# One more gate unit ahead of the delta heads of a hybrid attention and DeltaNet block, and its logits over more rounds

## What is computed

```python
h    = rmsnorm(x, pre_norm_gain) * (1 + scale) + shift          # scale, shift, gate from c @ w_ada
proj = h @ w_in                                                  # 1024 x 10840
# branch A: 8 heads of 128; an indexer of 8 heads of 64 picks 128 keys per query
score = einsum(w_idx, relu(q_idx @ k_idx.T * 64**-0.5)) ; causal ; top 128
y_a  = (softmax(q @ k.T over the chosen keys) @ v * silu(az)) @ w_a_out
# branch B: gated DeltaNet, 8 heads of 128, causal conv of width 4, silu, l2norm
y_b  = (rmsnorm(delta_rule(q, k, v, g, beta)) * silu(bz)) @ w_b_out
y    = sigmoid(ga) * y_a + sigmoid(gb) * y_b
out  = x + gate * rmsnorm(y @ w_o, post_norm_gain)
```

## Time and profile before

| | us |
|---|---|
| median of three runs | 810.59 |
| the profiled execution | 810.23 |
| its span, first to last instruction | 808.3 |
| TensorE busy | 776.9 |
| VectorE busy | 445.3 |
| ScalarE busy | 336.3 |
| GpSimd busy | 398.1 |
| granted TensorE clock, mean | 0.995 |

### The profile page before, as it was taken

How to read it: one execution, slowest core, us unless ns; L and a number is a source line. 1 busy time by engine, 2 the same in 40 slices (tenths; PEclk the granted TensorE clock), 3 DMA queues, 4 the chain that set the end, 5 groups by cost and what they waited for, 6 DMA issues and landing times.

```text
span 808.3 us, 11722 instructions
## 1 busy us (share of the span) xinstructions
PE 776.9 (96%) x4288; PEld 628.5 (78%) x4288; DVE 445.3 (55%) x998; ACT 336.3 (42%) x719; POOL 398.1 (49%) x348
## 2 busy tenths in 40 slices
PE   4998998999999899999999999999999999999997
PEld 4877875677877688878888777778777788878997
DVE  5858778767588977878754243243334233331114
ACT  5576544533544345444344433443432332222131
POOL 3665542365545455565435255365355355434451
PEclk9999999999999999999999999999999999999999
DMA  8945555433344142323122121222132245432602
GB/s 326 415 153 192 161 102 199 109 120 105 99 93 107 66 112 92 105 66 117 57 76 78 53 78 54 78 79 76 55 103 69 90 163 179 153 130 83 230 1 105
DMA packets 69496, 95.55 MB, mean 118 GB/s; under 512 B 32936, under 2 KB 45608, under 8 KB 69440
## 3 DMA queue, kind: packets, MB, share of 16 engines
q1 hardware_dynamic: 69440, 94.81, 36.0%
HBM read 85.02 MB, written 9.22 MB: 117 GB/s over the span
## 4 chain that ended last, share of the span: by engine, by line
PE 79%; DVE 10%; ACT 4%; DMA 3%; issue 2%; POOL 1%; SPq 1%; DVEq 0%; POOLq 0%; ACTq 0%
PE ps L735 19%; PE ps L737 18%; PE ps L736 18%; PE ps L1025 2%; PE ps L1079 2%; PE ps L1078 2%; PE ps L1077 2%; PE ps L1012 2%; ACT prob L1346 2%; DVE prob L1989 1%; DVE binv L1876 1%; DMA mod_rows<-in_w_mod 1%; PE ps L1019 1%; PE ps L867 1%; PE ps L852 1%
## 5 line engine op out<-in xcount | busy, mean ns | idle before, releaser
L1444 POOL TENSOR_TENSOR w_lo<-raw,w_hi 128x512 fp32r<-128x512 f32 x210 | 282.0, 1366 | 295.0 <-ACT w_hi L1097 294.9
L735 PE MATMUL ps<-h_hi,w_hi 128*128 128x512 f32 x648 | 274.9, 424 | 0.0
L737 PE MATMUL ps<-h_hi,w_lo 128*128 128x512 f32 x648 | 254.6, 393 | 0.0
L736 PE MATMUL ps<-h_lo,w_hi 128*128 128x512 f32 x648 | 254.0, 392 | 0.0
L735 PEld LDWEIGHTS ps<-h_hi,w_hi 128*128 128x128 f32 x648 | 122.5, 189 | 30.3 <-issue 9.1
L737 PEld LDWEIGHTS ps<-h_hi,w_lo 128*128 128x128 f32 x648 | 122.1, 188 | 27.5
L736 PEld LDWEIGHTS ps<-h_lo,w_hi 128*128 128x128 f32 x648 | 122.8, 190 | 22.0 <-issue 2.2
L1097 ACT ACTIVATE w_hi<-raw 128x1024 fp32r<-128x1024 f32 x105 | 109.6, 1054 | 17.1 <-PE ps L1079 17.1
L1282 ACT ACTIVATE o_tok<-ps 128x128 f32<-128x128 f32 x32 | 8.9, 277 | 90.5 <-PE ps L977 90.4
L1994 DVE SCALAR_TENSOR_TENSOR oat<-ps,za 128x512 f32<-128x512 f32 x8 | 5.5, 691 | 56.1 <-PE ps L1025 56.1
L1078 PE MATMUL ps<-w_lo,y_hi 128*128 128x256 f32 x128 | 36.2, 283 | 0.0
(11 more groups left out here) (280 smaller groups left out, 1367.9 us busy)
## 6 DMA issues: line engine op xcount, KB each, us to landing
raw<-in_w_units SPq DMA_DIRECT2D x105, 512.0 KB, 3.3
mod_rows<-in_w_mod SPq DMA_DIRECT2D x16, 512.0 KB, 8.7
inverse_tiles<-zero SPq DMA_DIRECT2D x12, 344.0 KB, 5.0
ada<-in_w_gate SPq DMA_DIRECT2D x8, 512.0 KB, 4.5
x_sb<-in_x SPq DMA_DIRECT2D x4, 512.0 KB, 6.1
first_raw<-in_w_first SPq DMA_DIRECT2D x8, 256.0 KB, 7.3
L<-gc_rows SPq DMA_DIRECT2D x8, 256.0 KB, 3.9
lower_tiles<-L SPq DMA_DIRECT2D x8, 256.0 KB, 2.3
```

The lines of the kernel that those rows point to most:

```text
L735: pe.matmul(out_ap, w_hi[:, slot, k, :], rhs_hi(k), start=(k == 0), stop=False)
L736: pe.matmul(out_ap, w_hi[:, slot, k, :], rhs_lo(k), start=False, stop=False)
L737: mm = pe.matmul(out_ap, w_lo[:, slot, k, :], rhs_hi(k), start=False, stop=(k == KT - 1))
L1444: ins = pool.tensor_tensor(w_lo[:, slot, ks], raw[:, slot, ks], w_hi[:, slot, ks].bitcast(F32), ALU.subtract)
```

## The change

`N_EARLY` goes from 5 to 6: GA 5 stands ahead of delta head 0, in rounds 52 to 55, and all of `R_DELTA` grows by 4 (52 to 56, ..., 164 to 168). With it go K 7, the grams of heads 4 to 7, the second inverse and its corner steps, the selection, `R_ROPE[0]` (151 to 155), `R_MASK` and `R_ATT[0]` to `R_ATT[2]` (192, 202, 212 to 196, 206, 216). The number of rounds, the units from AQ 1 on and `R_ATT[3]` on, the other ropes, and everything up to round 49 but the logits keep their rounds.

The extra units behind the heads are K 7, GA 6, GA 7, AV 0, AQ 0, AK 0, AZ 0 instead of K 7, GA 5, GA 6, GA 7, AQ 0, AK 0, AV 0, with AZ 0 behind head 7. AZ 0 so goes from rounds 176 to 179 to 164 to 167, AV 0 from 160 to 163 to 116 to 119.

The 12 pairs of logits go from rounds 38, 39, 40, 41, 43, 44, 45, 46, 48, 49, 50, 52 to 38, 39, 41, 42, 44, 45, 47, 48, 50, 51, 53, 55. The load of `P_b` for head 0 goes from round 47 to 51, that of the first inverse from 52 to 54.

```diff
-N_EARLY = 5
-MIDDLE = [("K", 4), ("GA", 0), ("K", 5), ("GA", 1), ("K", 6), ("GA", 2), ("GA", 3), ("GA", 4)]
-EXTRA = ([("K", 7)] + [("GA", n) for n in range(N_EARLY, KT)] + [("AQ", 0), ("AK", 0), ("AV", 0), ("AZ", 0)])[:HEADS - 1] + [None]
+N_EARLY = 6
+MIDDLE = [("K", 4), ("GA", 0), ("K", 5), ("GA", 1), ("K", 6), ("GA", 2), ("GA", 3), ("GA", 4), ("GA", 5)]
+EXTRA = ([("K", 7)] + [("GA", n) for n in range(N_EARLY, KT)] + [("AV", 0), ("AQ", 0), ("AK", 0), ("AZ", 0)])[:HEADS - 1] + [None]
...
-R_LOGIT = [R_DELTA[0] - 14 + 14 * (m // 2) // 11 for m in range(24)]
+R_LOGIT = [R_DELTA[0] - 18 + 17 * (m // 2) // 11 for m in range(24)]
```

## The result

Over 20 runs of each kernel the changed one has a median of 812.81 us (810.64 to 817.31), the one before 810.47 us (809.05 to 812.49). The ratio is 1.0035, 95% interval [1.0023, 1.0047]: slower by 0.35%, 2.8 us (the two medians stand 2.3 apart). The profiled execution of the changed kernel took 814.17 us, with a span of 812.3, so it stands 1.4 us above its median, where the profiled execution of before stood near its own.

The account below looks back on a forecast made before the run. TensorE, busy 776.9 of 808.3 us, was the bound; only gaps and slow clock could change. Terms 0.1 + 0.5 + 0.4 + 0.1 + 0.9 = +2.0 on 810.23 gave 812.2, stated as 812.4; range 811.0 to 813.4, eight in ten 808.8 to 814.3.

Parts of the forecast that it names:

- gaps at the logits: TensorE's three waits for VectorE's scoring, 3.07 us together, fall to between 0 and 0.6; 0 taken.
- end of corner step 7: On VectorE, this step ends at 144.2 (142.4 to 145.1) instead of 150.48.
- from there to the gram: From corner step 7's end through DMA queue, GpSimd and ScalarE to kd, ahead of head 4's gram: 12.9 us.
- gap before the gram: TensorE, due at 153.9, waits for kd until 157.1 before head 4's gram: 3.2 us (1.4 to 4.1).
- lost to the slow clock in this stretch: A half-speed stretch behind the gap before the gram costs 1.7 us, as one did behind the earlier 2.00 us gap.
- K1 of head 6 (AZ 0): AZ 0's VectorE product at round 168 delays the selection and makes K1 wait 0.5 us (0 to 0.6).
- rope 1 at head 7: Rope 1 at round 191, now between st2 and r3, costs 0.4 us (0 to 1.1), GpSimd's half included.
- rope 2 at attention 1: Rope 2 at round 207, between attention 1's second and third row maximum on VectorE, adds 0.9 us (0 to 1.1).
- The query decay: Head 0's P_b load falls behind the corner stores on the DMA queue, delaying kd; TensorE waits 3.2 us at head 4's gram.
- (a): Faster side: P_b barely late, a gap of 1.1 at head 4's gram, no slow clock; 808.4 or median 808.8; chance 0.17.
- (b): Neighbours' slack hides the three tail costs: 810.3 to 811, no change; chance 0.25.
- (c): The moved 2.04 us gap at head 2 is followed by a slow stretch: +1.7, 814.1; chance 0.18.

Follow-up runs that it names:

- experiment 3: Changed kernel with head 0's P_b load back in round 47, ahead of the corner stores, and ropes 1 and 2 four rounds later: 805.94 us, ratio 0.9948.
- 10: The same kernel as experiment 3, run again beside 9 on one chip: 806.12 us, ratio 0.9941 to the kernel before.
- 1: Changed kernel with only head 0's P_b load put back in round 47, ahead of the corner stores: 809.69 us, ratio 0.9991 to the kernel before.
- 4: Kernel before with only head 0's P_b load moved behind the corner stores, in round 50: 819.84 us, ratio 1.0117.
- experiment 5: Changed kernel with ropes 1 and 2 four rounds later and P_b left late: 809.44 us, ratio 0.9994 to the kernel before.
- 9: Kernel before with only the logit pairs respread, over rounds 38 to 52: 805.71 us, ratio 0.9943.
- 6: Changed kernel with P_b early and rope 2 alone four rounds later: 806.68 us, ratio 0.9955 to the kernel before.
- experiment 2: Changed kernel with the logit pairs kept in rounds 38 to 52, as before: 819.70 us, ratio 1.0114 to the kernel before.
- 7: Changed kernel with P_b early and the logit pairs kept in rounds 38 to 52: 814.55 us, ratio 1.0048 to the kernel before.
- 8: Changed kernel with P_b early, ropes 1 and 2 four rounds later and rope 0 in round 182: 805.43 us, ratio 0.9941 to before.

## Why the prediction was right, by its steps

The sum said 812.2 for an execution and 812.4 as a median; it was 814.2 and 812.8, slower as forecast and for the reason given. The agreement of the medians is closer than that of the terms. Term by term, in the profiled execution:

| term | forecast, us | measured, us |
|---|---|---|
| gaps at the logits | 0 (0 to 0.6) | 1.11 |
| end of corner step 7 | 144.2 | 144.97 |
| from there to the gram | 12.9 | 13.4 |
| gap before the gram | 3.2 | 3.52 |
| lost to the slow clock in this stretch | 1.7 | 3.0 |
| K1 of head 6 (AZ 0) | 0.5 | 0.31 |
| rope 1 at head 7 | 0.4 | 1.13 |
| rope 2 at attention 1 | 0.9 | 1.10 |
| AZ 1 at attention 0 | 0.1 | 0 |
| gaps in heads 1 and 2 | 0 | -1.6 |
| first logit products reached | 0 | -0.5 |

The last two rows: the gaps of 1.04 at 251.6 and 1.15 at 279.0 before are 0.23 and 0.40 after, and TensorE came to the logits at 114.32 instead of 114.84. Together: 1.11 + 3.52 - 3.07 = 1.56 for the gaps, 3.0 - 1.7 = 1.3 for the clock, 2.54 for the tail, less 1.56 and less 0.5, are 3.3; the spans differ by 4.0, and the 0.7 between is not assigned.

Luck has a part. The gap before the gram came out within 0.3 because both of its ends were late, TensorE by 1.0 (154.9 for 153.9) and `kd` by 1.3 (158.4 for 157.1). The 1.6 us that heads 1 and 2 gave back stand in no term of the forecast; without them the profiled execution would have stood at 815.7. The two gaps together are 0.6 to 1.6 us in the seven profiles with the changed kernel's rounds for the logits and 1.6 to 2.6 in the other five, so they may hang on the change, but they also differ within one kernel (1.25 in experiment 3, 0.70 in 10). Their cause is open.

Of the signs that the forecast named, the gap before the gram, its chain and the 2.2 us at attention 1 came as said; K1 of head 6 waited 0.31 and not half a microsecond, and the logits kept a gap over 0.6.

**The query decay** was right in place and order and near in size, and experiments 1 and 4 show it from both sides. The chain was 0.5 longer than summed because P_b took 4.25 us to land and be used instead of 3.76.

**The logits.** The step that failed here is "the three gaps fall to between 0 and 0.6": one of 1.11 stayed. VectorE in the changed kernel (the counterpart of the earlier trace rows), and beside it the same step in experiment 5:

```profile
120.79 2.31 DVE L1800 SCALAR_TENSOR_TENSOR kraw<-ps,pcol,kraw 128x511 f32<-128x511 f32 x3 [1.46 <-ACT kraw L1195]
...
123.70 1.75 DVE L1876 TENSOR_TENSOR binv<-pair_c,pair_a 128x512 f32<-128x512 f32 x1 [0.59 <-DMA pair_b<-inverse_tiles]
```

```profile
121.18 2.31 DVE L1801 SCALAR_TENSOR_TENSOR kraw<-ps,pcol,kraw 128x511 f32<-128x511 f32 x3 [1.45 <-ACT kraw L1196]
...
123.41 0.68 DVE L1877 TENSOR_TENSOR binv<-pair_c,pair_a 128x512 f32<-128x512 f32 x1
```

The taps began at 120.8, earlier than the 121.4 forecast, but corner step 0 then waited 0.59 for its DMA and ran beside GpSimd's split, 1.75 instead of 0.68, and pair 2 ended 1.1 late. In experiment 5 the same instruction met neither and pair 4 waited for nothing. Which it is varies from execution to execution: experiments 3 and 10 are the same kernel, the first without this gap, the second with 1.11. So 1.1 belonged in the bounds. The forecast also took 1.52 as the longest such product; that was the longest of eight (those from `pair_c`), and one from `pair_b` took 1.75 before too. The two waits met took 1.75 and 1.79.

**Rope 1** was mis-sized by 0.7. The sum followed VectorE: `r3` a little late, V3 not at all, as it turned out. The gap came on GpSimd (the first four lines are the changed kernel's, the last the kernel before's):

```profile
435.28 3.43 POOL L1532 TENSOR_TENSOR qk<-qk,tab_cos 32x1024 f32<-32x1024 f32 x1 [2.16 <-DVE sw L1955]
...
438.68 3.50 POOL L1444 TENSOR_TENSOR w_lo<-raw,w_hi 128x512 fp32r<-128x512 f32 x2
...
442.15 0.19 POOL L1526 TENSOR_TENSOR fo<-fo,kst 128x4 f32<-128x4 f32 x1
...
438.74 2.30 DVE L1962 TENSOR_TENSOR qk<-qk,sw 32x1024 f32<-32x1024 f32 x1 [1.15 <-POOL qk L1532]
...
435.35 2.38 POOL L1532 TENSOR_TENSOR qk<-qk,tab_cos 32x1024 f32<-32x1024 f32 x1
```

Its half of the rope took 3.43 us, where before it took 2.38 and stood behind head 7's norm. Now it stands ahead and pushed the split of a unit, and that ran for 3.50 instead of 2.54 because VectorE's last step of the rope (2.30 instead of 1.21) ran beside it; head 7's norm is queued behind, at 442.15, 1.4 us after ScalarE was done with what it needs. By the Trainium skill, SBUF — State Buffer, section "Who interferes with whom", a VectorE instruction with both inputs in SBUF and a GpSimd instruction that reads SBUF exclude each other; the trace agrees, both being stretched by about a microsecond. The forecast named GpSimd's half of the rope but put only "as much again" for it, 0.2, which left this out.

**Rope 2 and AZ 0** were right in mechanism and within 0.2. No experiment moves AZ 0 back, but its gap, 0.30 or 0.31, stands in all nine profiles with the new order of units and in none of the three with the old (before, 4 and 9).

**The rivals.** (a), the faster side, asked for a gap of 1.1 and no slow clock; the chain took 13.4 us, and neither happened. (b), tail costs hidden, fell: all three showed up, and experiments 3, 5 and 6 take two of them away again. (c), a slow stretch at head 2, did not happen in the profiled execution of the changed kernel: its gap of 2.07 was followed by none. As a matter of the execution it is borne out: behind the gap of 2.0 to 2.1 us at head 2 the clock fell in six of the twelve profiled executions of these kernels (experiments 1, 2, 4, 5, 6 and 7) and stayed in six (before, after, 3, 8, 9 and 10), with the same instructions before it. The gap of head 1 shortly ahead of it does not decide: it was 0.2 to 1.1 us in the first six and 0.2 to 1.7 in the others. The Trainium skill, TensorE: Matmul & The Clock Gate, section "What's actually happening", has the clock's watching run on from one execution to the next, by which the same gap costs in one and not in another; the traces fit that, six to six. The 20 times of the changed kernel spread over 6.7 us and those of before over 3.4. The four longest of the 20 (816.4 to 817.3) have a mean granted clock of 0.981 to 0.986, the four shortest (810.6 to 811.4) one of 0.990 to 0.994, so slow stretches go with the long times; that they make up all of the difference is not shown.

## What to carry to other kernels

In a kernel driven by a time table, a step that keeps its distance to the work it serves may still change its place in a queue: look at what waits ahead of it on its DMA queue before looking at its engine. Shift the dense stretch itself before shifting what stands around it; here the twelve rounds of one list were worth 4.6 us, and moving everything else by a unit to make room cost more than that, by the query decay (3.6 us) and the two ropes (3.3). A gap removed is worth its own length plus the clock behind it, and the second part comes by chance.

## What the hardware showed that was not expected

The clock's half speed after a stall is not a fixed price: 3.4 us of it followed 2.00 us gaps at the logits in all four profiled kernels that have them (before and experiments 2, 4 and 7) and the gap of 2.98 in experiment 2, none followed one of 2.49 (experiment 5), and two gaps of 1.1 within two microseconds brought it in experiments 1 and 7 but not in the changed kernel or experiment 2. With the gaps of 3.52 and 6.33 came 6.8 us of it, which began inside the gap; only the part in which TensorE had work cost time, 6.1 and 3.0 us at half speed. So the longer stall did not have the dearer clock.

The front varies too. Up to round 38 the twelve kernels are the same, and TensorE came to the first logit products at 113.86 to 115.57. In five of the twelve (experiments 2, 4, 6, 7 and 10) the clock was granted at 0.50 for 10.2 us from about 16 us on; these came to the logits at 115.1 to 115.6, the others at 113.9 to 115.3.

Two kernels whose gaps differ by 2 us can so differ by 4 or by nothing in single executions. That this is why the medians of experiments 1 to 3 add up to no better than about 2 us is argued, not shown.
